# Weighted sum of gathered expert rows: from diagonal matmuls on TensorE to two running sums on VectorE

## The chip, the core and the metric

The kernel runs on one core of a Trainium2 chip. The metric is the device time of one execution in microseconds (us), lower is better. Four engines matter here: TensorE (PE, with its weight loads as PEld), VectorE (DVE), ScalarE (ACT) and GpSimd (POOL). POOL issues the indirect DMAs that gather rows.

## What is computed

Two transformer blocks on 512 tokens of width 1024, in fp32. The change sits in the last part of the first block, a mixture of single-neuron experts (PEER). For each token, product keys pick 8 x 16 = 128 experts with gates; then a dot product with each expert's U row, a gelu, and a weighted sum of the experts' V rows:

```python
def expert_block(args):
    hb, eb, gb = args
    a = jax.nn.gelu(jnp.einsum('td,ted->te', hb, u_tab[eb]).astype(jnp.float32), approximate=False)
    w = (gb * a).astype(hb.dtype)
    return jnp.einsum('te,ted->td', w, v_tab[eb])
```

Every (token, expert) pair needs its own U row and V row: 512 x 128 pairs with 8 KB each.

## The kernel before

The kernel is a row of stages; stage_peer is the one that changes. Tokens are worked on in TB = 4 blocks of P = 128, a token per partition. A block has SLOTS = 128 slots, one for each expert of a token, so there are 512 slots n in all. For slot n one indirect DMA gathers 128 rows of the joined U and V table (1 MB) into entry n % 12 of `uv_ring`; U is the first half of the entry and V the second. The order on each engine is written out by hand and ordered by semaphores:

- **POOL** (L1177 to L1186) issues gather n when s_pv says that slot n - 12 has been added, so its ring entry is free.
- **VectorE** (L1287 to L1305), in each slot n: waits for the gather, multiplies U by the token's row and reduces to one number (L1295, the dot, with a second short instruction that reads the accumulator). In slots with n % 4 = 1 it multiplies the four gelus of the group before by their gates (`weigh`, L1274). Then come a few instructions of the *routing* of the next block (`route`, L1193 to L1260: top-16 searches, and one-hot products of 128x2048 at L1247 to L1253), spread over the first 88 slots of blocks 0 to 2. `gates` (L1262) follows in slot 110, and `update` (L1276), which adds the previous block's result to the residual, in slot 10.
- **ScalarE** (L1327 to L1343), for each group of four slots: the gelu of four dots, then four diagonal matrices `expert_diag` (L1338: identity times the weight column), in a ring of 8.
- **TensorE** (L1366 to L1377), for each slot: two matmuls of diagonal by V (L1372) accumulate in two PSUM banks. The last one releases the ring entry (s_pv). At a block's end ScalarE copies the banks to `out_rows` (L1323), TensorE turns them (L1362), and VectorE's `update` takes the turned tiles from PSUM.

After stage_peer comes the second block of the network (norm, projections, attention, FFN), which needs the last block's `update`.

Of the kernel before, what the change touches and what calls it, by code (L numbers as in the profile page):

```python
# [14 lines left out]
ALU = mybir.AluOpType  # L15
ACT = mybir.ActivationFunctionType
AX_X = mybir.AxisListType.X

P = 128
S = 512  # L20
D = 1024
KD = D // P
TB = S // P
# [9 lines left out]
SLOTS = PEER_H * TOPK  # L33
# [1084 lines left out]
def stage_peer(K):  # L1118
# [3 lines left out]
    nc = K.nc  # L1122
    NT = 2 * PEER_H
    RING = 12
    G = 4
    NGRP = SLOTS // G
    DIAGS = 8
    ROUTE_SLOTS = 88
    EXP_GROUP = 26
    TAIL_SLOT = 110  # L1130
    OUT_SLOT = 10
    with ExitStack() as ctx:
        ring = K.sb(ctx, "uv_ring", [P, RING, 2 * D])
        hN = K.sb(ctx, "h_rows", [P, TB, D])
        xin = K.sb(ctx, "x_again", [P, KD, S])
        oN = K.sb(ctx, "out_rows", [P, D])
# [14 lines left out]
        a = [K.sb(ctx, f"expert_dot{i}", [P, SLOTS]) for i in range(2)]  # L1151
        gl = [K.sb(ctx, f"expert_gelu{i}", [P, SLOTS]) for i in range(2)]
        w = [K.sb(ctx, f"expert_weight{i}", [P, SLOTS]) for i in range(2)]
        diag = [K.sb(ctx, f"expert_diag{i}", [P, P]) for i in range(DIAGS)]
        s_sw = [K.sem(f"route_scores_landed{i}") for i in range(2)]
        s_swf, s_x = K.sem("route_scores_used"), K.sem("x_landed_again")
        s_ht, s_he = K.sem("h_turned"), K.sem("h_rows_copied")
        s_dve, s_d, s_e = K.sem("route_dve"), K.sem("route_diff"), K.sem("route_exp")
        s_idx, s_gate = K.sem("indices_ready"), K.sem("gates_ready")
        s_land = [K.sem(f"rows_landed{r}") for r in range(RING)]  # L1160
        s_dot, s_gelu, s_w, s_diag, s_pv = (
            K.sem("expert_" + n) for n in ("dots", "gelus", "weights", "diagonals", "added"))
        s_oe, s_ot, s_y = K.sem("out_rows_copied"), K.sem("out_turned"), K.sem("x_updated")
        block = ctx.enter_context(nc.Block())

        @block.sync
        def _(sp):
            for tb in range(TB):
                if tb >= 2:
                    sp.wait_ge(s_swf, tb - 1)  # L1170
                sp.dma_start(sw[tb % 2][:, :, :], K.s_dram[tb]).then_inc(s_sw[tb % 2], 16)
                if tb == 1:
                    sp.dma_start(xin[:, :, :], K.x_dram.rearrange("k p s -> p k s")).then_inc(s_x, 16)
# [15 lines left out]
        def _(dve):  # L1189
# [72 lines left out]
            def gates(tb):  # L1262
                dve.wait_ge(s_e, tb + 1)
                g = gate[tb % 2][:, :].rearrange("p (h a) -> p h a", h=PEER_H)
                ch.link(dve.tensor_reduce(den[:, :], g, AX_X, ALU.add))
                ch.link(dve.reciprocal(den[:, :], den[:, :]))
                dve.tensor_tensor(g, g, den[:, :].unsqueeze(2).to_broadcast([P, PEER_H, TOPK]), ALU.mult).then_inc(s_gate, 1)

            def weigh(n):
                tb, g = divmod(n, NGRP)  # L1270
                c = slice(g * G, g * G + G)
                dve.wait_ge(s_gelu, n + 1)
                dve.wait_ge(s_gate, tb + 1)
                dve.tensor_tensor(w[tb % 2][:, c], gl[tb % 2][:, c], gate[tb % 2][:, c], ALU.mult).then_inc(s_w, 1)  # L1274

            def update(tb):  # L1276
                c = slice(tb * P, (tb + 1) * P)
                dve.wait_ge(s_ot, tb + 1)
                if tb == 0:
                    dve.wait_ge(s_x, 16)  # L1280
                for k in range(KD):
                    dve.scalar_tensor_tensor(out=K.hT[:, k, c], in0=K.ps[4 + k // 4][:, (k % 4) * P:(k % 4 + 1) * P],
                                             scalar=K.modT[:, M_GATE2 + k:M_GATE2 + k + 1], in1=xin[:, k, c],
                                             op0=ALU.mult, op1=ALU.add).then_inc(s_y, 1)
            steps = sum(1 for _ in route(0))
            gates(0)
            for tb in range(TB):  # L1287
                ahead, done = (route(tb + 1) if tb + 1 < TB else iter(())), 0
                for s in range(SLOTS):
                    n = tb * SLOTS + s  # L1290
                    if s == 0:
                        dve.wait_ge(s_he, 2 * (tb + 1))
                    dve.wait_ge(s_land[n % RING], 16 * (n // RING + 1))
                    u = ring[:, n % RING, 0:D]
                    dve.tensor_tensor_reduce(u, u, hN[:, tb, :], 1.0, 0.0, ALU.mult, ALU.add,  # L1295
                                             a[tb % 2][:, s:s + 1]).then_inc(s_dot, 1)
                    if n % G == 1 and n > G:
                        weigh(n // G - 1)
                    while done * ROUTE_SLOTS < steps * (s + 1) and done <= steps:
                        next(ahead, None)  # L1300
                        done += 1
                    if s == TAIL_SLOT and tb + 1 < TB:
                        gates(tb + 1)
                    if s == OUT_SLOT and tb:
                        update(tb - 1)  # L1305
            weigh(TB * NGRP - 1)
            update(TB - 1)

        @block.scalar
        def _(act):  # L1310
            def rows(tb):
                for half in range(2):
                    act.wait_ge(s_ht, 2 * tb + half + 1)
                    act.copy(hN[:, tb, 512 * half:512 * half + 512], K.ps[4 + 2 * (tb % 2) + half][:, :]).then_inc(s_he, 1)

            def exps(tb):
                act.wait_ge(s_d, tb + 1)
                act.activation(gate[tb % 2][:, :], top[:, :, :].rearrange("p a b -> p (a b)"), ACT.Exp).then_inc(s_e, 1)

            def out(tb):  # L1320
                act.wait_ge(s_pv, (tb + 1) * SLOTS)
                for half in range(2):
                    act.copy(oN[:, 512 * half:512 * half + 512], K.ps[2 * (tb % 2) + half][:, :]).then_inc(s_oe, 1)  # L1323
            for tb in range(TB):
                rows(tb)
            exps(0)
            for n in range(TB * NGRP):  # L1327
                tb, g = divmod(n, NGRP)
                c = slice(g * G, g * G + G)
                act.wait_ge(s_dot, G * (n + 1))  # L1330
                act.activation(gl[tb % 2][:, c], a[tb % 2][:, c], ACT.Gelu).then_inc(s_gelu, 1)  # L1331
                act.wait_ge(s_w, n + 1)
                for j in range(G):
                    q = n * G + j
                    if q >= DIAGS:
                        act.wait_ge(s_pv, q - DIAGS + 1)
                    s = g * G + j
                    act.activation(diag[q % DIAGS][:, :], K.ident[:, :], ACT.Copy,  # L1338
                                   scale=w[tb % 2][:, s:s + 1]).then_inc(s_diag, 1)
                if g == EXP_GROUP and tb + 1 < TB:  # L1340
                    exps(tb + 1)
                if g == 0 and tb:
                    out(tb - 1)  # L1343
            out(TB - 1)

        @block.tensor
        def _(pe):
            for tb in range(TB):
                for half in range(2):
                    if tb >= 2:  # L1350
                        pe.wait_ge(s_he, 2 * (tb - 2) + half + 1)
                    for k in range(4):
                        last = nc.tensor.transpose(K.ps[4 + 2 * (tb % 2) + half][:, k * P:(k + 1) * P],
                                                   K.hT[:, 4 * half + k, tb * P:(tb + 1) * P], K.ident[:, :])
                    last.then_inc(s_ht, 1)

            def turn(tb):
                pe.wait_ge(s_oe, 2 * (tb + 1))
                if tb:
                    pe.wait_ge(s_y, KD * tb)  # L1360
                for k in range(KD):
                    last = nc.tensor.transpose(K.ps[4 + k // 4][:, (k % 4) * P:(k % 4 + 1) * P],  # L1362
                                               oN[:, k * P:(k + 1) * P], K.ident[:, :])
                last.then_inc(s_ot, 1)
            pe.wait_ge(s_he, 2 * TB)
            for n in range(TB * SLOTS):  # L1366
                tb, s = divmod(n, SLOTS)
                if s == 0 and tb >= 2:
                    pe.wait_ge(s_oe, 2 * (tb - 1))
                pe.wait_ge(s_diag, n + 1)  # L1370
                for half in range(2):
                    last = nc.tensor.matmul(K.ps[2 * (tb % 2) + half][:, :], diag[n % DIAGS][:, :],  # L1372
                                            ring[:, n % RING, D + 512 * half:D + 512 * half + 512],
                                            start=s == 0, stop=s == SLOTS - 1)
                last.then_inc(s_pv, 1)
                if s == G - 1 and tb:
                    turn(tb - 1)  # L1377
            turn(TB - 1)


def stage_in2(K):
# [682 lines left out]
```

## Time and profile before

| | us |
|---|---|
| median of 3 runs (lowest to highest) | 3002.18 (2997.97 to 3004.06) |
| profiled execution, its own time | 2998.2 |
| its span in the trace | 2996.5 |
| first dot starts, last dot starts | 744.2, 2038.1 |
| busy in the whole span: PE, DVE, ACT, POOL | 2280.6, 1359.5, 643.1, 804.3 |

The stage between the first and the last dot takes 1293.9 of the 2996.5 us. The page of the profile gives for each group of instructions the busy time, the mean of one in ns, and the idle time of its engine just before, with what ended it. An engine's busy share over the span says little: stages differ in what limits them.

### The profile page before, as it was taken

Reading aid. Unit: us, or ns where it says so; the run is one execution under the profiler, and the core shown is the slowest. Engines: PE = TensorE matmul, PEld = TensorE weight load, DVE = VectorE, ACT = ScalarE, POOL = GpSimd, SP = SyncE. Lnnn points to the kernel's source line nnn. Section 1 sums busy time; section 2 is a strip of 40 time slices with the busy share of each in tenths; the row PEclk is TensorE's granted clock in tenths of the full one; section 3 lists DMA queues with packets and bytes.
Section 4 is the critical chain, followed back from the end, with each engine's and each line's share of the span. In section 5 each row is a group of like instructions: output and inputs, shape, how many; then the busy total and the mean of one; then the engine's idle time right before and its main releaser. Section 6 shows DMA issues by size and latency. Waiting matters only on the chain. (4 is left out here: it accounts for less than half of the span.)

```text
span 2996.5 us, 21852 instructions
## 1 busy us (share of the span) xinstructions
PE 2280.6 (76%) x6939; PEld 1232.1 (41%) x6939; DVE 1359.5 (45%) x2853; ACT 643.1 (21%) x1374; POOL 804.3 (27%) x618
## 2 busy tenths in 40 slices
PE   4896698670777788777877778785985496799979
PEld 1344343560233333333332333332662242488767
DVE  1107441317667566765677554554144563222200
ACT  1202240200111111112111111113112352255411
POOL 1000000221444444444444444340310000144342
PEclk8897699895899999989899998997996598899989
DMA  6100251333999999999999999993220001133242
GB/s 212 51 14 0 64 162 58 98 91 128 421 420 420 412 420 420 420 386 420 420 420 388 420 420 420 420 420 114 70 88 0 0 1 42 56 98 91 77 116 66
DMA packets 234190, 656.48 MB, mean 219 GB/s; under 512 B 15953, under 2 KB 156796, under 8 KB 168060
## 3 DMA queue, kind: packets, MB, share of 16 engines
q0 software_dynamic: 73728, 536.90, 43.3%
q1 hardware_dynamic: 150416, 110.50, 11.9%
q10 hardware_dynamic: 9966, 8.12, 0.9%
q8 instruction: 36, 0.59, 0.1%
q14 instruction: 44, 0.36, 0.0%
HBM read 645.76 MB, written 9.72 MB: 219 GB/s over the span
## 5 line engine op out<-in xcount | busy, mean ns | idle before, releaser
L1372 PE MATMUL ps<-uv_ring,expert_diag 128*128 128x512 f32 x2048 | 1002.0, 647 | 359.5 <-ACT expert_diag L1338 359.5
L1295 DVE CUSTOM_DVE_ANT_0 uv_ring<-uv_ring,h_rows 128x1024 f32<-128x1024 f32 x512 | 628.9, 1230 | 494.4 <-DMA uv_ring<-in_peer_uv_dram,expert_idx 493.5
L1372 PEld LDWEIGHTS ps<-uv_ring,expert_diag 128*128 128x128 f32 x2048 | 412.5, 207 | 946.5 <-issue 568.5
L1183 POOL DMA_INDIRECT uv_ring<-in_peer_uv_dram,expert_idx x512 | 562.3, 1098 | 814.0 <-PE ps L1372 702.6
L1338 ACT ACTIVATE expert_diag<-ident,expert_weight 128x128 f32<-128x128 f32 x512 | 163.5, 390 | 626.7 <-DVE expert_weight L1274 626.7
L271 POOL TENSOR_TENSOR ffn_low<-ffn_raw,ffn_high 128x1024 fp32r<-128x1024 f32 x44 | 105.2, 2393 | 520.8 <-ACT ffn_high L260 520.8
L271 POOL TENSOR_TENSOR peerq_low<-peerq_raw,peerq_high 128x1024 fp32r<-128x1024 f32 x16 | 38.0, 2380 | 550.8 <-ACT peerq_high L260 550.8
L115 PE MATMUL ps<-ffn_h_high,ffn_high 128*128 128x512 f32 x352 | 139.6, 397 | 18.4 <-POOL ffn_low L271 18.3
L117 PE MATMUL ps<-ffn_h_high,ffn_low 128*128 128x512 f32 x352 | 137.6, 391 | 0.0
L116 PE MATMUL ps<-ffn_h_low,ffn_high 128*128 128x512 f32 x352 | 137.6, 391 | 0.0
L1331 ACT ACTIVATE expert_gelu<-expert_dot 128x4 f32<-128x4 f32 x128 | 26.3, 205 | 490.1 <-DVE expert_dot L1295 490.1
L110 PE MATMUL ps<-hT,in_w 128*128 128x512 f32 x192 | 85.2, 607 | 10.7 <-ACT hT L164 10.7
L1897 DVE TENSOR_TENSOR ffn_prod<-ffn_silu,ps 128x512 f32<-128x512 f32 x22 | 15.2, 689 | 166.4 <-PE ps L117 166.4
L115 PE MATMUL ps<-ff_high,down_high 128*128 128x512 f32 x176 | 69.3, 394 | 20.1 <-POOL down_low L271 20.1
L115 PEld LDWEIGHTS ps<-ffn_h_high,ffn_high 128*128 128x128 f32 x352 | 66.4, 189 | 40.1 <-issue 27.0
L271 POOL TENSOR_TENSOR in_low<-in_raw,in_high 128x1024 fp32r<-128x1024 f32 x16 | 40.8, 2557 | 147.7 <-ACT in_high L260 147.7
L110 PE MATMUL ps<-mix2T,out_w 128*128 128x512 f32 x128 | 56.9, 608 | 22.6 <-DMA out_w<-in_w_out_dram 22.6
L117 PEld LDWEIGHTS ps<-ffn_h_high,ffn_low 128*128 128x128 f32 x352 | 66.5, 189 | 14.2
L116 PEld LDWEIGHTS ps<-ffn_h_low,ffn_high 128*128 128x128 f32 x352 | 66.5, 189 | 13.1
L271 POOL TENSOR_TENSOR down_low<-down_raw,down_high 128x2816 fp32r<-128x2816 f32 x8 | 49.8, 6234 | 78.3 <-ACT down_high L260 78.3
L116 PE MATMUL ps<-ff_low,down_high 128*128 128x512 f32 x176 | 69.0, 392 | 0.0
L117 PE MATMUL ps<-ff_high,down_low 128*128 128x512 f32 x176 | 69.0, 392 | 0.0
(323 smaller groups left out, 2833.5 us busy)
## 6 DMA issues: line engine op xcount, KB each, us to landing
wada_rest<-in_w_ada_dram SPq DMA_DIRECT2D x16, 1024.0 KB, 5.2
ffn_raw<-in_w_gate_dram SPq DMA_DIRECT2D x22, 512.0 KB, 3.8
ffn_raw<-in_w_up_dram SPq DMA_DIRECT2D x22, 512.0 KB, 3.9
down_raw<-in_w_down_dram SPq DMA_DIRECT2D x8, 1408.0 KB, 7.1
wada<-in_w_ada_dram SPq DMA_DIRECT2D x4, 2048.0 KB, 9.5
out_w<-in_w_out_dram SPq DMA_DIRECT2D x8, 1024.0 KB, 5.3
peerq_raw<-in_w_peer_q_dram SPq DMA_DIRECT2D x16, 512.0 KB, 4.0
uv_ring<-in_peer_uv_dram,expert_idx POOLq DMA_INDIRECT x512, 13.7
```

The lines of the kernel that those rows point to most:

```text
L110: return nc.tensor.matmul(out, lhsT, rhs, start=first, stop=last)
L115: nc.tensor.matmul(out, w[0], x[0], start=first, stop=False)
L116: nc.tensor.matmul(out, w[0], x[1], start=False, stop=False)
L117: return nc.tensor.matmul(out, w[1], x[0], start=False, stop=last)
L271: pool.tensor_tensor(self.lo[s][:, :, :], self.raw[s][:, :, :], self.hi[s][:, :, :].bitcast(F32), ALU.subtract).then_inc(self.s_lo[s], 1)
L1183: pool.indirect_dma_start(out=ring[:, n % RING, :], out_offset=None, in_=K.uv, in_offset=bass.IndirectOffsetOnAxis(ap=idx[tb % 2][:, s:s + ...
L1295: dve.tensor_tensor_reduce(u, u, hN[:, tb, :], 1.0, 0.0, ALU.mult, ALU.add, a[tb % 2][:, s:s + 1]).then_inc(s_dot, 1)
L1331: act.activation(gl[tb % 2][:, c], a[tb % 2][:, c], ACT.Gelu).then_inc(s_gelu, 1)
L1338: act.activation(diag[q % DIAGS][:, :], K.ident[:, :], ACT.Copy, scale=w[tb % 2][:, s:s + 1]).then_inc(s_diag, 1)
L1372: last = nc.tensor.matmul(K.ps[2 * (tb % 2) + half][:, :], diag[n % DIAGS][:, :], ring[:, n % RING, D + 512 * half:D + 512 * half + 512], ...
L1897: dve.tensor_tensor(prod[:, :], sl[:, :], K.ps[1][:, :], ALU.mult).then_inc(s_prod, 1)
```

## The change

The diagonals, their matmuls and the PSUM sums go. In their place VectorE itself multiplies each V row by its weight and adds it to one of two SBUF sums (even slots to one, odd slots to the other), five slots behind the dot (LAG = 5). The first add of each sum is a plain multiplication (`tensor_scalar`). After a block's last add VectorE adds the two sums into `out_rows`, and TensorE turns those as before. `update` moves from slot 10 to slot 16. The add, not the matmul, now releases the ring entry to POOL.

```diff
-    DIAGS = 8
+    LAG = G + 1
...
-    OUT_SLOT = 10
+    OUT_SLOT = 16
...
-        diag = [K.sb(ctx, f"expert_diag{i}", [P, P]) for i in range(DIAGS)]
+        acc = [K.sb(ctx, f"expert_sum{i}", [P, D]) for i in range(2)]
...
+            def add(n):
+                tb, s = divmod(n, SLOTS)
+                v, x = ring[:, n % RING, D:2 * D], w[tb % 2][:, s:s + 1]
+                dve.wait_ge(s_w, n // G + 1)
+                if s < 2:
+                    if tb:
+                        dve.wait_ge(s_oe, tb)
+                    ins = dve.tensor_scalar(acc[s % 2][:, :], v, x, None, ALU.mult)
+                else:
+                    dve.wait_ge(s_pv, n - 1)
+                    ins = dve.scalar_tensor_tensor(out=acc[s % 2][:, :], in0=v, scalar=x, in1=acc[s % 2][:, :],
+                                                   op0=ALU.mult, op1=ALU.add)
+                ins.then_inc(s_pv, 1)
+                if s == SLOTS - 1:
+                    if tb:
+                        dve.wait_ge(s_ot, tb)
+                    dve.wait_ge(s_pv, n + 1)
+                    dve.tensor_tensor(oN[:, :], acc[0][:, :], acc[1][:, :], ALU.add).then_inc(s_oe, 1)
+
...
                     if n % G == 1 and n > G:
                         weigh(n // G - 1)
+                    if n >= LAG:
+                        add(n - LAG)
...
             weigh(TB * NGRP - 1)
+            for n in range(TB * SLOTS - LAG, TB * SLOTS):
+                add(n)
             update(TB - 1)
...
-                act.wait_ge(s_w, n + 1)
-                for j in range(G):
-                    q = n * G + j
-                    if q >= DIAGS:
-                        act.wait_ge(s_pv, q - DIAGS + 1)
-                    s = g * G + j
-                    act.activation(diag[q % DIAGS][:, :], K.ident[:, :], ACT.Copy,
-                                   scale=w[tb % 2][:, s:s + 1]).then_inc(s_diag, 1)
...
-            for n in range(TB * SLOTS):
-                tb, s = divmod(n, SLOTS)
-                if s == 0 and tb >= 2:
-                    pe.wait_ge(s_oe, 2 * (tb - 1))
-                pe.wait_ge(s_diag, n + 1)
-                for half in range(2):
-                    last = nc.tensor.matmul(K.ps[2 * (tb % 2) + half][:, :], diag[n % DIAGS][:, :],
-                                            ring[:, n % RING, D + 512 * half:D + 512 * half + 512],
-                                            start=s == 0, stop=s == SLOTS - 1)
-                last.then_inc(s_pv, 1)
```

VectorE's queue in four slots of the routing part of a block, before (L1295 is the dot and its accumulator read, L1274 is `weigh`, L1204 and L1212 to L1220 are routing):

```order
L1204 MAX_INDEX route_idx<-route_max,route_scores 128x8 x2
L1295 ISA uv_ring,expert_dot<-uv_ring,h_rows 128x1024
L1295 ISA expert_dot 128x1
L1274 TENSOR_TENSOR expert_weight<-expert_gelu,expert_gate 128x4
L1204 MAX_INDEX route_idx<-route_max,route_scores 128x8
L1295 ISA uv_ring,expert_dot<-uv_ring,h_rows 128x1024
L1295 ISA expert_dot 128x1
L1204 MAX_INDEX route_idx<-route_max,route_scores 128x8
```

The same kind of place now (L1313 is the dot, L1273 `weigh`, L1285 the add, L1224 and L1230 routing):

```order
L1313 ISA uv_ring,expert_dot<-uv_ring,h_rows 128x1024
L1313 ISA expert_dot 128x1
L1285 SCALAR_TENSOR_TENSOR expert_sum<-uv_ring,expert_weight,expert_sum 128x1024
L1230 MATCH_REPLACE route_cand<-route_top,route_cand 128x256 x2
L1313 ISA uv_ring,expert_dot<-uv_ring,h_rows 128x1024
L1313 ISA expert_dot 128x1
L1273 TENSOR_TENSOR expert_weight<-expert_gelu,expert_gate 128x4
L1285 SCALAR_TENSOR_TENSOR expert_sum<-uv_ring,expert_weight,expert_sum 128x1024
L1230 MATCH_REPLACE route_cand<-route_top,route_cand 128x256
```

Each slot has gained one VectorE instruction of 128x1024 between its dot and its routing work. At the end of the stage VectorE's queue now reads as follows (L1292 adds the two sums, L1300 is `update`):

```order
L1313 ISA uv_ring,expert_dot<-uv_ring,h_rows 128x1024
L1313 ISA expert_dot 128x1
L1285 SCALAR_TENSOR_TENSOR expert_sum<-uv_ring,expert_weight,expert_sum 128x1024
L1273 TENSOR_TENSOR expert_weight<-expert_gelu,expert_gate 128x4
L1285 SCALAR_TENSOR_TENSOR expert_sum<-uv_ring,expert_weight,expert_sum 128x1024 x5
L1292 TENSOR_TENSOR out_rows<-expert_sum 128x1024
L1300 SCALAR_TENSOR_TENSOR hT<-ps,modT,x_again 128x128 x8
```

Before, nothing but `weigh` and the eight of `update` stood behind the last dot on this engine. On TensorE the stage changes like this:

```order
-L1353 MATMUL ps<-ident,hT 128x128 x32
-L1372 MATMUL ps<-uv_ring,expert_diag 128x512 x264
-L1362 MATMUL ps<-ident,out_rows 128x128 x8
-L1372 MATMUL ps<-uv_ring,expert_diag 128x512 x256
-L1362 MATMUL ps<-ident,out_rows 128x128 x8
...
+L1360 MATMUL ps<-ident,hT 128x128 x32
+L1370 MATMUL ps<-ident,out_rows 128x128 x32
```

Only the turning of rows stays on TensorE during the stage.

## Rows read from the trace of the kernel before

**Rows 1.** Page, groups of instructions: busy, mean ns | idle before, releaser.

```profile
L1372 PE MATMUL ps<-uv_ring,expert_diag 128*128 128x512 f32 x2048 | 1002.0, 647 | 359.5 <-ACT expert_diag L1338 359.5
L1295 DVE CUSTOM_DVE_ANT_0 uv_ring<-uv_ring,h_rows 128x1024 f32<-128x1024 f32 x512 | 628.9, 1230 | 494.4 <-DMA uv_ring<-in_peer_uv_dram,expert_idx 493.5
L1183 POOL DMA_INDIRECT uv_ring<-in_peer_uv_dram,expert_idx x512 | 562.3, 1098 | 814.0 <-PE ps L1372 702.6
```

**Rows 2.** Stretches of the stage: PE, PEld, DVE, ACT, POOL busy, PEclk, DMA share, GB/s.

```profile
1000.00:1100.00 100.00, 78.35 (x168) 32.81 (x168) 56.20 (x120) 18.66 (x55) 41.51 (x40) 0.93 1.01 420
1300.00:1400.00 100.00, 79.90 (x163) 33.27 (x164) 54.00 (x103) 18.98 (x57) 43.34 (x40) 0.91 0.97 397
1600.00:1700.00 100.00, 76.65 (x158) 32.16 (x159) 64.36 (x109) 17.71 (x53) 45.40 (x39) 0.90 0.97 396
```

**Rows 3.** Timeline of DVE, four dots: start, us, instruction, idle before and releaser.

```profile
1499.56 1.23 DVE L1295 CUSTOM_DVE_ANT_0 uv_ring<-uv_ring,h_rows 128x1024 f32<-128x1024 f32 x1 [0.78 <-DMA uv_ring<-in_peer_uv_dram,expert_idx]
...
1507.04 1.23 DVE L1295 CUSTOM_DVE_ANT_0 uv_ring<-uv_ring,h_rows 128x1024 f32<-128x1024 f32 x1 [0.69 <-DMA uv_ring<-in_peer_uv_dram,expert_idx]
```

**Rows 4.** Timeline of DVE where landed rows had piled up.

```profile
1303.50 1.22 DVE L1295 CUSTOM_DVE_ANT_0 uv_ring<-uv_ring,h_rows 128x1024 f32<-128x1024 f32 x1
1304.65 0.08 DVE L1295 DVE_READ_ACCUMULATOR2_ANT expert_dot<- 128x1 f32 x1
1304.65 1.22 DVE L1295 CUSTOM_DVE_ANT_0 uv_ring<-uv_ring,h_rows 128x1024 f32<-128x1024 f32 x1
...
1306.94 0.15 DVE L1274 TENSOR_TENSOR expert_weight<-expert_gelu,expert_gate 128x4 f32<-128x4 f32 x1
1307.02 1.22 DVE L1295 CUSTOM_DVE_ANT_0 uv_ring<-uv_ring,h_rows 128x1024 f32<-128x1024 f32 x1
```

**Rows 5.** DVE instructions nearest to the add: groups and one merged timeline row.

```profile
2068.68 5.39 DVE L158 SCALAR_TENSOR_TENSOR X<-hT,vecT,rs_in 128x512 f32<-128x512 f32 x8
L158 DVE SCALAR_TENSOR_TENSOR X<-hT,vecT,rs_in x8: 743/744/750, 2068.7 to 2073.3; 128x512 f32<-128x512 f32 x8
L727 DVE TENSOR_TENSOR gla_qe<-qkT,gla_e x7: 1208/1216/1224, 256.1 to 289.5; 128x1024 f32<-128x1024 f32 x7
L311 DVE TENSOR_TENSOR ffn_h_low<-hT,ffn_h_high 128x512 fp32r<-128x512 f32 x8 | 4.9, 686 | 0.9 <-ACT ffn_h_high L306 0.9
L934 DVE TENSOR_SCALAR swa_p<-swa_p,swa_sum x32: 346/351/354, 357.7 to 436.3; 128x256 f32<-128x256 f32 x32
```

**Rows 6.** DVE groups in 975.5:1301, block 1 from its first dot.

```profile
L1295 DVE CUSTOM_DVE_ANT_0 uv_ring<-uv_ring,h_rows 128x1024 f32<-128x1024 f32 x128 | 157.2, 1230 | 109.8 <-DMA uv_ring<-in_peer_uv_dram,expert_idx 109.7
L1265 DVE TENSOR_REDUCE route_den<-expert_gate 128x8 f32<-128x128 f32 x1 | 0.3, 286 | 0.5 <-ACT expert_gate L1318 0.5
```

**Rows 7.** Timeline: a routing step that waits for the one before it.

```profile
1300.67 0.29 DVE L1258 SCALAR_TENSOR_TENSOR expert_idxf<-route_e 128x128 f32<-128x128 f32 x1
1301.00 0.23 DVE L1260 CAST expert_idx<-expert_idxf 128x128 uint32<-128x128 f32 x1
```

**Rows 8.** The gather's source line on POOL: ns min/median/max, and issue to landing.

```profile
L1183 POOL DMA_INDIRECT uv_ring<-in_peer_uv_dram,expert_idx x512: 935/940/3040, 736.6 to 2022.4; - x171
DMA to landing us min/median/max: 5.6/13.7/20.5
```

**Rows 9.** Timelines of POOL and DVE: gathers issued during VectorE's work.

```profile
882.51 1.43 POOL L1183 DMA_INDIRECT uv_ring<-in_peer_uv_dram,expert_idx  x1 [5.43 <-PE ps L1372]
...
881.90 1.23 DVE L1295 CUSTOM_DVE_ANT_0 uv_ring<-uv_ring,h_rows 128x1024 f32<-128x1024 f32 x1 [0.99 <-DMA uv_ring<-in_peer_uv_dram,expert_idx]
883.06 2.29 DVE L1212 TENSOR_TENSOR route_cand<-route_max 128x2048 f32<-128x2048 f32 x1
...
1282.10 3.04 POOL L1183 DMA_INDIRECT uv_ring<-in_peer_uv_dram,expert_idx  x1 [1.78 <-PE ps L1372]
...
1282.04 2.29 DVE L1247 TENSOR_TENSOR route_scores<-route_cf,iota 128x2048 f32<-128x2048 f32 x1
...
1504.56 0.94 POOL L1183 DMA_INDIRECT uv_ring<-in_peer_uv_dram,expert_idx  x1 [0.47 <-PE ps L1372]
...
1504.54 1.27 DVE L1295 CUSTOM_DVE_ANT_0 uv_ring<-uv_ring,h_rows 128x1024 f32<-128x1024 f32 x1 [1.05 <-DMA uv_ring<-in_peer_uv_dram,expert_idx]
```

**Rows 10.** Timelines of ACT, PE and DVE at the stage's end.

```profile
2048.96 1.07 ACT L1323 COPY out_rows<-ps 128x512 f32<-128x512 f32 x2 [7.88 <-PE ps L1372]
2050.08 1.09 PE L1362 MATMUL ps<-ident,out_rows 128*128 128x128 f32 x8 [1.17 <-ACT out_rows L1323]
2051.21 2.16 DVE L1282 SCALAR_TENSOR_TENSOR hT<-ps,modT,x_again 128x128 f32<-128x128 f32 x8 [11.45 <-PE ps L1362]
```

**Rows 11.** Stretches with an idle PE, PE alone: busy, PEclk, DMA share, GB/s.

```profile
690.00:740.00 50.00, 0.00 (x0) 0.50 0.10 34
2050.00:2052.00 2.00, 1.09 (x8) 1.00 0.00 0
2055.40:2057.00 1.60, 1.60 (x2) 0.50 0.94 204
```

More of the change, by code:

```diff
@@ L1160, in stage_peer @@
         s_land = [K.sem(f"rows_landed{r}") for r in range(RING)]
-        s_dot, s_gelu, s_w, s_diag, s_pv = (
-            K.sem("expert_" + n) for n in ("dots", "gelus", "weights", "diagonals", "added"))
-        s_oe, s_ot, s_y = K.sem("out_rows_copied"), K.sem("out_turned"), K.sem("x_updated")
+        s_dot, s_gelu, s_w, s_pv = (K.sem("expert_" + n) for n in ("dots", "gelus", "weights", "added"))
+        s_oe, s_ot, s_y = K.sem("out_rows_summed"), K.sem("out_turned"), K.sem("x_updated")
         block = ctx.enter_context(nc.Block())
@@ L1318, in exps @@
                 act.activation(gate[tb % 2][:, :], top[:, :, :].rearrange("p a b -> p (a b)"), ACT.Exp).then_inc(s_e, 1)
-            def out(tb):
-                act.wait_ge(s_pv, (tb + 1) * SLOTS)
-                for half in range(2):
-                    act.copy(oN[:, 512 * half:512 * half + 512], K.ps[2 * (tb % 2) + half][:, :]).then_inc(s_oe, 1)
             for tb in range(TB):
@@ L1331, in _ @@
                 act.activation(gl[tb % 2][:, c], a[tb % 2][:, c], ACT.Gelu).then_inc(s_gelu, 1)
-                act.wait_ge(s_w, n + 1)
-                for j in range(G):
-                    q = n * G + j
-                    if q >= DIAGS:
-                        act.wait_ge(s_pv, q - DIAGS + 1)
-                    s = g * G + j
-                    act.activation(diag[q % DIAGS][:, :], K.ident[:, :], ACT.Copy,
-                                   scale=w[tb % 2][:, s:s + 1]).then_inc(s_diag, 1)
                 if g == EXP_GROUP and tb + 1 < TB:
                     exps(tb + 1)
-                if g == 0 and tb:
-                    out(tb - 1)
-            out(TB - 1)
         @block.tensor
@@ L1355, in _ @@
                     last.then_inc(s_ht, 1)
-            def turn(tb):
-                pe.wait_ge(s_oe, 2 * (tb + 1))
+            pe.wait_ge(s_he, 2 * TB)
+            for tb in range(TB):
+                pe.wait_ge(s_oe, tb + 1)
                 if tb:
@@ L1364, in turn @@
                 last.then_inc(s_ot, 1)
-            pe.wait_ge(s_he, 2 * TB)
-            for n in range(TB * SLOTS):
-                tb, s = divmod(n, SLOTS)
-                if s == 0 and tb >= 2:
-                    pe.wait_ge(s_oe, 2 * (tb - 1))
-                pe.wait_ge(s_diag, n + 1)
-                for half in range(2):
-                    last = nc.tensor.matmul(K.ps[2 * (tb % 2) + half][:, :], diag[n % DIAGS][:, :],
-                                            ring[:, n % RING, D + 512 * half:D + 512 * half + 512],
-                                            start=s == 0, stop=s == SLOTS - 1)
-                last.then_inc(s_pv, 1)
-                if s == G - 1 and tb:
-                    turn(tb - 1)
-            turn(TB - 1)
 def stage_in2(K):
```

## The prediction

> **What bounds the stage now.** I read the page's groups first. The diagonal matmuls are the costliest group of the whole program, with 1002.0 us busy, and that invites the guess that taking them away gains much. The idle column says otherwise [rows 1]: VectorE's dots waited 493.5 us, all of it for gathers; POOL waited 702.6 us for the matmuls, which is no more than a full ring. The stretches settle it [rows 2]: the DMA engines are busy all the time (share 1.01, 420 GB/s), with two dips to 0.97. In steady state three dots are 7.48 us apart, 2.49 us a slot [rows 3], and 1 MB at 420 GB/s is 2.5 us. So DMA bandwidth bounds the stage, and 512 slots x 2.49 = 1275 of its 1293.9 us are bandwidth. Nothing that TensorE gives back can make it shorter. What matters is whether VectorE, which had 110 us of slack in a block of 325.5 us [rows 6], can carry the adds below the 2.49.
>
> **VectorE's new load.** I count by pitch (start to start), since instructions overlap: an instruction's duration is some 0.08 more than its pitch.
> - A dot: with rows piled up, 1303.50 to 1304.65, pitch 1.15 with its accumulator read; `weigh` has 0.08 [rows 4]. Over the three dots from 1303.50 to 1306.94 it is 1.147, which I use.
> - An add: scalar_tensor_tensor of 128x1024 from SBUF isn't in the trace. The same operation at 128x512 takes 744 ns, and eight take 5.39, so its pitch is (5.39 - 0.74) / 7 = 0.664 [rows 5]. From 512 to 1024 elements tensor_tensor goes from 686 to 1216 ns, 0.53 more. So the add has a pitch of 0.664 + 0.53 = 1.20. Bounds: below, the tensor_tensor of 128x1024, 1.216 - 0.08 = 1.14; above, two of 128x512, 1.33. I take 1.20, since the operation is the same and the slope is plain. The first add of each sum is a tensor_scalar: 351 ns for 256 elements where tensor_tensor would have some 0.42, so it runs at two elements at a time; I put it at 0.67, eight times.
> - `weigh` is now followed by an add that needs its result. A step that waits for the one before starts 0.33 after it where that took 0.29 [rows 7], so `weigh` (0.16) costs 0.20 in place of 0.08: 0.12 more, in every fourth slot.
> - The final addition of a block: 1.22 less the overlap, with the wait in front some 1.33.
>
> A slot without routing is thus 1.147 + 1.20 + 0.20 / 4 = 2.40 us, just below DMA's 2.49. With routing it is above.
>
> **Other work on VectorE.** Block 1 lasts 325.5 us from its first dot, less 110.3 idle = 215.2 occupied [rows 6]. Less 128 dots (146.8) and less some 10 for the overlap that a queue without gaps saves (0.08 in each slot), 58 are left for routing, `weigh` issue, `update` and `gates`. In the 88 routing slots that is near 0.6 a slot: 3.0 us against DMA's 2.49. So blocks 0 to 2 become VectorE's.
>
> **The sum from the first dot to the last.** 511 dots x 1.147 = 586.1; 506 adds (498 x 1.20 + 8 x 0.67) = 603.0; other work 3 x 58 = 174, less an `update` that block 0 lacks (2.1), plus `weigh` and `update` of block 3 (4.7) = 176.6; waits behind `weigh` 127 x 0.12 = 15.2; three final additions 4.0. Together 1384.9. The first five slots have no add and stay with DMA: 5 x (2.49 - 1.75) = +3.7. At the other end, from slot 88 of block 2 on, 168 slots have no routing and DMA is the slower by 0.09 to 0.10 each, 16.3. The rows landed ahead pay part of it: a ring entry is released 2.35 after the dot five slots on has started, the issue may have to wait some 1.1 for a dot (below), and issue to landing takes at least 5.6 [rows 8], so gather n + 12 lands some 9.0 after dot n + 5 starts, and is needed 7 slots or 16.8 after: 7.8 to spare. VectorE's final addition, `update` and `gates` there (4.5) count against it too, so 16.3 - 7.8 - 4.5 = +4. Sum: 1392.6 against 1293.9, **+98.7**.
>
> **The end.** Before, 13.1 us from the last dot's start (2038.1) to `update` (2051.21): TensorE worked off its backlog, ScalarE copied the banks, TensorE turned them in 1.09 [rows 10]. Now: dot 1.15, add 1.20, `weigh` 0.20, five adds 6.0, final addition 1.33, and the turning. TensorE has rested by then, and in a stretch without matmuls its granted clock is 0.50, that is 1.2 in place of 2.4 GHz, where the turning before had 1.00 [rows 11]; so I double it to 2.2, with 0.1 of handing over. 12.2 us: **-0.9**. The matmuls that come next started at 0.50 before as well [rows 11], so nothing changes for them. Turnings of blocks 0 to 2 have eleven slots of cover before `update`. ScalarE's lost 164 us were covered by the DMA wait and give nothing; its gelus can only come sooner.
>
> +98.7 - 0.9 = +97.8 on the profiled 2998.2 gives 3096. The runs' median is 4 above the profiled execution: **3100 us**.
>
> **A rule weighed.** VectorE and POOL meet [rows 9]. A gather issued during a dot (882.51, dot until 883.13) ends at 883.94, 0.81 after the dot, in place of taking 0.94; one issued at 1282.10 under a routing product until 1284.33 ends at 1285.14, again 0.81 after. The median issue is 940 ns, the longest 3040 [rows 8]. So POOL waits for a VectorE instruction with two SBUF inputs to end, and it slips in between that and the next, even where they overlap (883.06). In the other direction the dot of 1504.54, begun with a gather's issue, took 1.27 in place of 1.23. Hence now: an entry is released at an add's end, the issue is held by the following dot and ends about 2.0 after the release, inside the 2.4 of a slot. VectorE loses at most 0.04 a slot, 20 us in all if it always met; this is part of my upper bound.
> The Trainium skill's page "SBUF — State Buffer", section "SBUF: two separate sides", says that whichever of the two starts first has the shared pair for its whole instruction and the other fully blocks. For POOL waiting the trace agrees; for VectorE waiting it shows 0.04 and not the 0.94 of an issue. By that rule each issue could stop VectorE for some 0.8 us.
>
> **Rivals.**
> 1. *Adds hidden, on the other side: no change or a small gain.* If the add ran like the tensor_scalar (0.67), a slot would be 1.147 + 0.67 + 0.05 = 1.87, with routing 2.5 on average, and DMA would bind everywhere. Then the two dips (3% of 100 us each) and some 3 us at the end come back: about 2994. It decides if the pitch of an add is below about 0.75. Against it: 744 ns for 512 elements of the same operation [rows 5]. 3%.
> 2. *VectorE stopped by each issue* (the lock in both directions): 512 x 0.8 = 410, about 3510. Against it: the dot that met an issue took 1.27, not 2.0 [rows 9]. 3%.
> 3. *POOL starved.* Between an add and the next dot there is no accumulator read; if POOL could not slip in there or missed its one gap, an issue would wait for two instructions, as the 3.04 of 1282.10 [rows 9], and the 3.5 us period would outlast the slot in the 248 slots without routing. With a pace between 2.4 and 3.5, say 3.0: 248 x 0.6 = 149, about 3250. 6%.
> 4. *Dearer adds or stretched dots*: pitch 1.33 gives 498 x 0.13 = 65 less the 4 at the end, 3160; stretched dots give 3120. 12%.
> The rest, 76%, is the forecast. Its own range: with adds at 1.14 VectorE saves 30, but DMA then binds more at the end (168 x 0.16 = 27, less 7 and 4.5, is 15 in place of 4), so 3081; above, 3130.
>
> **Range and chances.** 3070 to 3165 takes in the forecast, both bounds of the add and rival 4; rivals 1 to 3 stay outside with 12%. About 0.2% (6 us) is what a measurement of this kernel tells from no change. Slower: rivals 2 to 4 and the forecast, 97%; rival 1 is split, 1% faster and 2% the same.
>
> **What would show it.** Right: add rows of about 1.28 us; in the first 88 slots of blocks 0 to 2 no idle time before dots and a slot of 3.0, DMA share there near 0.83; later slots at 2.40, turning to 2.49 with waits for DMA late in block 3; POOL issues near 2.0 us; granted clock 0.50 throughout. Wrong: adds of 0.7 us (rival 1), VectorE instructions of about 2 us (rival 2), or dots that wait for gathers while the DMA share is well below 1 (rival 3).

## The result

| | us |
|---|---|
| before, median of 4 runs (lowest to highest) | 3001.53 (2997.97 to 3004.06) |
| changed kernel, median of 4 runs (lowest to highest) | 3100.82 (3098.41 to 3101.39) |
| ratio, 95% interval | 1.033 (1.0312 to 1.0348) |
| forecast | 3100 (3070 to 3165), slower with 97% |
| profiled execution, its own time and span | 3101.39, 3099.6 |

The kernel became 3.3% slower, as forecast. The page of the changed kernel, its groups of instructions (busy, mean ns | idle before, releaser), beside [rows 1]:

```profile
L1182 POOL DMA_INDIRECT uv_ring<-in_peer_uv_dram,expert_idx x512 | 788.1, 1539 | 693.2 <-DVE expert_sum L1285 574.3
L1285 DVE SCALAR_TENSOR_TENSOR expert_sum<-uv_ring,expert_weight,expert_sum 128x1024 f32<-128x1024 f32 x504 | 645.1, 1281 | 4.4
L1313 DVE CUSTOM_DVE_ANT_0 uv_ring<-uv_ring,h_rows 128x1024 f32<-128x1024 f32 x512 | 621.5, 1214 | 18.7 <-DMA uv_ring<-in_peer_uv_dram,expert_idx 14.9
L1370 PE MATMUL ps<-ident,out_rows 128*128 128x128 f32 x32 | 7.8, 426 | 1460.4 <-DVE out_rows L1292 1460.4
```

Read the idle columns. The dots' wait for gathers has gone from 493.5 to 14.9 us: VectorE is now the engine that is waited for. TensorE's 1002 us of matmuls are gone and the engine idles; no time came back for it. The stretches of block 2's routing part, of its other 40 slots, and of block 3 (PE, PEld, DVE, ACT, POOL busy, PEclk, DMA share, GB/s), beside [rows 2]:

```profile
1462.70:1724.40 261.70, 1.97 (x8) 1.57 (x8) 260.43 (x501) 4.52 (x22) 127.86 (x89) 0.50 0.95 365
1724.40:1823.50 99.10, 0.00 (x0) 0.00 (x0) 98.61 (x136) 4.93 (x13) 64.13 (x40) 0.50 0.96 391
1823.50:2141.90 318.40, 1.97 (x8) 1.57 (x8) 311.14 (x424) 6.37 (x31) 209.74 (x122) 0.50 0.99 412
```

In the first, VectorE is busy for 260.43 of 261.70 us and the gathers come at 365 in place of 420 GB/s. From the dots' starts in the timeline: the routing parts of blocks 0 to 2 take 257.7, 261.6 and 261.6 us where they took 227.4, 228.5 and 228.1; the 40 slots behind each take 99.2 against 97.1 to 97.4. Block 3, during which VectorE has no routing to do, takes the same 318.4 from first to last dot in both kernels. So all of the loss, 103.0 us between first and last dot, lies in blocks 0 to 2.

The timeline of VectorE in slots without routing, and then POOL's row there:

```profile
1402.23 1.22 DVE L1313 CUSTOM_DVE_ANT_0 uv_ring<-uv_ring,h_rows 128x1024 f32<-128x1024 f32 x1
1403.38 0.08 DVE L1313 DVE_READ_ACCUMULATOR2_ANT expert_dot<- 128x1 f32 x1
1403.38 1.28 DVE L1285 SCALAR_TENSOR_TENSOR expert_sum<-uv_ring,expert_weight,expert_sum 128x1024 f32<-128x1024 f32 x1
1404.58 1.22 DVE L1313 CUSTOM_DVE_ANT_0 uv_ring<-uv_ring,h_rows 128x1024 f32<-128x1024 f32 x1
...
1402.59 1.68 POOL L1182 DMA_INDIRECT uv_ring<-in_peer_uv_dram,expert_idx  x1 [0.67 <-DVE expert_sum L1285]
```

Dot pitch 1.15, add pitch 1.20, no gap. The add before this dot ended at 1402.32; the issue starts 0.27 later, is held until the dot ends at 1403.45, and ends 0.82 behind it, still inside the slot's 2.35.

At the stage's end (DVE and PE timelines), beside [rows 10]:

```profile
2144.30 6.06 DVE L1285 SCALAR_TENSOR_TENSOR expert_sum<-uv_ring,expert_weight,expert_sum 128x1024 f32<-128x1024 f32 x5
2150.47 1.23 DVE L1292 TENSOR_TENSOR out_rows<-expert_sum 128x1024 f32<-128x1024 f32 x1
2153.76 2.16 DVE L1300 SCALAR_TENSOR_TENSOR hT<-ps,modT,x_again 128x128 f32<-128x128 f32 x8 [2.06 <-PE ps L1370]
...
2151.75 1.97 PE L1370 MATMUL ps<-ident,out_rows 128*128 128x128 f32 x8 [312.90 <-DVE out_rows L1292]
```

From the last dot (2141.9) to `update` 11.9 us, where it was 13.1. The turning took 1.97 in place of 1.09, at a granted clock of 0.50.

### The profile page after: what moved, and what is told of

Its sections match the earlier page's. It is cut to its first block and busy times, and to the rows that moved or that the text cites. A ratio compares the mean times of both kernels' runs of the same rounds, so it can differ in the third digit from the quotient of the medians.

```text
span 3099.6 us, 18137 instructions
## 1 busy us (share of the span) xinstructions
PE 1283.5 (41%) x4891; PEld 822.6 (27%) x4891; DVE 1943.4 (63%) x3369; ACT 475.4 (15%) x854; POOL 1030.1 (33%) x618
## 5 line engine op out<-in xcount | busy, mean ns | idle before, releaser
L1182 POOL DMA_INDIRECT uv_ring<-in_peer_uv_dram,expert_idx x512 | 788.1, 1539 | 693.2 <-DVE expert_sum L1285 574.3
L1285 DVE SCALAR_TENSOR_TENSOR expert_sum<-uv_ring,expert_weight,expert_sum 128x1024 f32<-128x1024 f32 x504 | 645.1, 1281 | 4.4
L1313 DVE CUSTOM_DVE_ANT_0 uv_ring<-uv_ring,h_rows 128x1024 f32<-128x1024 f32 x512 | 621.5, 1214 | 18.7 <-DMA uv_ring<-in_peer_uv_dram,expert_idx 14.9
L1370 PE MATMUL ps<-ident,out_rows 128*128 128x128 f32 x32 | 7.8, 426 | 1460.4 <-DVE out_rows L1292 1460.4
L1370 PEld LDWEIGHTS ps<-ident,out_rows 128*128 128x128 f32 x32 | 6.3, 223 | 1461.8 <-DVE out_rows L1292 1030.6
```

The lines of the kernel that those rows point to most:

```text
L1182: pool.indirect_dma_start(out=ring[:, n % RING, :], out_offset=None, in_=K.uv, in_offset=bass.IndirectOffsetOnAxis(ap=idx[tb % 2][:, s:s + ...
L1285: ins = dve.scalar_tensor_tensor(out=acc[s % 2][:, :], in0=v, scalar=x, in1=acc[s % 2][:, :], op0=ALU.mult, op1=ALU.add)
```

## Experiments

Two theories at first. **A**: VectorE's occupied time in the routing parts is the whole loss. **B**: the loss comes from the new path of release and issue, where most gathers' issues are held by a dot (the median one takes 1.68 in place of 0.94 us). Every kernel below starts from the changed kernel unless it says otherwise; each ratio is to the kernel before on the same chip.

**noroute** leaves out the routing of blocks 1 to 3, so that they work with block 0's experts and gates.

```diff
+                if tb:
+                    for _ in range(100):
+                        yield
+                    ch.link(dve.tensor_copy(cf[:, 0, 0:8], mif[:, 0, 0, 0:8]))
+                    dve.tensor_copy(cf[:, 0, 8:16], mif[:, 0, 0, 0:8]).then_inc(s_d, 1)
+                    dve.tensor_copy(cf[:, 0, 16:24], mif[:, 0, 0, 0:8]).then_inc(s_swf, 1)
+                    dve.wait_ge(s_swf, tb + 1)
+                    dve.tensor_copy(idx[tb % 2][:, :], idxf[:, :]).then_inc(s_idx, 1)
+                    return
```

> The changed kernel with the routing of blocks 1 to 3 left out (they use the experts and gates of block 0; four tiny copies keep the semaphores going). Adds, releases and gathers are as in the changed kernel. Theory A (VectorE's occupied time in the routing parts of blocks 0 to 2 is the whole loss): a slot needs 2.40 us of VectorE against 2.50 of DMA, so every block falls back to the 320 us of block 3 and the time to about 2987 us (2980 to 2994), a little below the kernel before. Theory B (the slower path of release and issue, gathers held up by VectorE's two-input instructions, is the loss): that path is untouched, so about 3100.

Measured: 2997.48 us, ratio 0.9986 (0.9977 to 0.9996). The whole loss is gone although all adds and the release path are there. The gather's source line and its landing times (ns min/median/max; us):

```profile
L1182 POOL DMA_INDIRECT uv_ring<-in_peer_uv_dram,expert_idx x512: 932/1786/1977, 736.7 to 2024.4; - x171
DMA to landing us min/median/max: 7.5/14.7/20.1
```

The issues are held as long as in the changed kernel (median 1786 against 1677 ns), and it costs nothing: theory B falls. The gathers of this kernel fetch the same rows in every block; width8 below does without that. A stretch of this kernel, its block 2:

```profile
1393.80:1718.05 324.25, 1.97 (x8) 1.57 (x8) 314.50 (x433) 9.45 (x35) 216.26 (x128) 0.50 1.01 416
```

DMA is busy throughout, and the block still takes 324 us, not the 320 I expected. So DMA's own pace is 324.25 / 128 = 2.53 a slot, not 2.49, and some 2997 us is what this way of gathering gives at DMA's pace. My 2987 (2980 to 2994) missed by that.

**width768, width512, width8** do the add on fewer columns; the rest of the sum is left out.

```diff
-                    ins = dve.scalar_tensor_tensor(out=acc[s % 2][:, :], in0=v, scalar=x, in1=acc[s % 2][:, :],
+                    ins = dve.scalar_tensor_tensor(out=acc[s % 2][:, 0:768], in0=v[:, 0:768], scalar=x, in1=acc[s % 2][:, 0:768],
```

> The changed kernel with each add done on 768 of its 1024 columns (the rest of the sum is left out). Theory A: the add's pitch falls by 256 x 1.04 ns = 0.27 to 0.93. The routing part of a block goes from 261.6 to 238 us, against DMA's 220; the 40 slots after it are DMA's (100) less some 8 for rows landed ahead, so a block takes 330, three take 991 against 975.5 before: 3014 us (3008 to 3025). Theory B: unchanged, since each release is still followed by a dot that holds the issue: near 3100.

> The changed kernel with each add done on 512 of its 1024 columns. Theory A: pitch 0.66, a routing slot 2.97 - 0.53 = 2.44, just under DMA's 2.50: the loss is gone, about 2991 us (2985 to 3000). Theory B: near 3100.

> The changed kernel with each add done on 8 of its 1024 columns, so that VectorE's load is nearly that of before, while TensorE still does no sums. Both theories: DMA bounds everything. Blocks near 320 us in place of 325, and an end that is shorter by six adds: about 2984 us (2978 to 2991). If it stayed at 3000 or above, something of the loss would come from TensorE's absence or from the order of releases.

| columns | us | ratio, 95% | routing part, block 2 | the 40 slots behind |
|---|---|---|---|---|
| 1024 | 3100.82 | 1.033 (1.0312 to 1.0348) | 261.6 | 99.2 |
| 768 | 3028.15 | 1.0093 (1.0076 to 1.011) | 240.4 | 96.5 |
| 512 | 3006.20 | 1.0023 (1.0013 to 1.0033) | 233.6 | 95.5 |
| 8 | 2997.07 | 0.9991 (0.9982 to 1.0001) | 231.3 | 95.1 |

From 1024 to 768 columns an add is 0.27 us shorter (1281 to 1014 ns), and 88 x 0.267 = 23 us a routing part are expected where 21 were measured: time follows VectorE's work nearly one for one. Further down it flattens: a routing part with the 40 slots behind it takes 329 and 326 us, near DMA's 324. The figures as expected were 14, 15 and 13 us too low, all three outside their ranges, in good part because a block needs 324 us of DMA and not 320.

The 2997 of width8 hides something. Its last dot starts at 2042.0, 3.9 us later than in the kernel before (2038.1), and its blocks 0 to 2 take 979.7 us (975.5 before, 973.7 in noroute); an end that is 5.7 us shorter, with its short adds, makes up for it. So VectorE's work is shown to be all but some 4 to 6 of the 103 us. What these few are, the 0.22 us that even an add of 8 columns takes, the order of the releases or something else, is open.

**tscalar** makes every add a tensor_scalar, without accumulation.

```diff
-                    ins = dve.scalar_tensor_tensor(out=acc[s % 2][:, :], in0=v, scalar=x, in1=acc[s % 2][:, :],
-                                                   op0=ALU.mult, op1=ALU.add)
+                    ins = dve.tensor_scalar(acc[s % 2][:, :], v, x, None, ALU.mult)
```

> The changed kernel with every add a tensor_scalar of all 1024 columns (the accumulation is left out): the price that the first rival put on the add. I expect 0.75 us for one, a pitch of 0.67, VectorE below DMA in every slot and about 2992 us (2985 to 3000). If an instruction that runs at two elements at a time kept POOL out for longer than its own duration, waits for gathers would appear and the time would be above 3010.

Measured: 3005.17 us, 1.0021 (1.0012 to 1.0031). Groups of this kernel:

```profile
L1285 DVE TENSOR_SCALAR expert_sum<-uv_ring,expert_weight 128x1024 f32<-128x1024 f32 x504 | 377.3, 749 | 4.4
```

and of width512:

```profile
L1285 DVE SCALAR_TENSOR_TENSOR expert_sum<-uv_ring,expert_weight,expert_sum 128x512 f32<-128x512 f32 x504 | 376.6, 748 | 4.4
```

The 2992 (2985 to 3000) expected was 13 us too low, as in width512 and for the same reason. Two different instructions of the same 0.75 us give the same time within some 1 us: what counts here is the duration on VectorE, and not whether the instruction reads one or two tensors from SBUF. It also shows that the first rival was a real one with a real price: with adds of pitch 0.67 the change would have cost 0.2% and not 3.3%, though it would not have gained (the rival had 2994).

**route112** spreads routing over 112 slots.

```diff
-    ROUTE_SLOTS = 88
-    EXP_GROUP = 26
-    TAIL_SLOT = 110
+    ROUTE_SLOTS = 112
+    EXP_GROUP = 29
+    TAIL_SLOT = 124
```

> The changed kernel with the routing spread over 112 in place of 88 slots of a block (exps and gates later too). Theory A says that the sum of VectorE's work in a block counts, 361 against 320 us, not its peaks: the same time, 3100 us (3095 to 3103), perhaps 2 less because only 144 in place of 168 slots without routing are left to DMA's slower pace. A theory by which the heaviest slots cost (the ring running empty there) expects a gain of 10 us or more.

Measured: 3096.45 us, 1.0325 (1.0308 to 1.0342). Blocks 1 and 2 take 361.1 us each, where they took 360.8 in the changed kernel. Where VectorE sets the pace throughout, only the sum of its work counts, not how it is spread. Of the 4 us that came back only 1.6 lie between first and last dot: block 3 takes 3.2 less (315.2), where 2 less were expected, and blocks 0 to 2 take 1.6 more. The others lie ahead of the first dot and behind the last.

**lag7, lag9** widen LAG; the diff of lag9 (lag7 has G + 3):

```diff
-    LAG = G + 1
+    LAG = G + 5
```

> The changed kernel with LAG = 7: five slots, 12.5 us, are left for the 9.0 of release, issue and landing, 3.5 us to spare in place of 8. The rows landed ahead that pay for the end are fewer, so DMA binds some 5 us earlier in block 3: 3106 us (3102 to 3115).

> The changed kernel with LAG = 9 in place of 5: an entry is released 9 slots behind its dot, so only 3 slots are left for issue and landing. By the sum of the prediction a gather lands 9.0 us after the dot with which its entry's release began, so 3 slots must last 9.0: a slot of 3.0 everywhere, also in the 248 slots without routing, 0.5 to 0.6 more each: about 3250 us (3220 to 3290). If release and issue had much more room than that sum says, the time would stay within 10 us of 3101.

Measured: lag7 3104.22 us, 1.0348 (1.0331 to 1.0365), as expected. lag9 3388.44, 1.1289 (1.127 to 1.1308), far above the 3250 (3220 to 3290) expected. Its source lines of the dot and the gather:

```profile
L1313 DVE CUSTOM_DVE_ANT_0 uv_ring<-uv_ring,h_rows x512: 1195/1224/1291, 745.0 to 2427.0; 128x1024 f32<-128x1024 f32 x171
...
L1182 POOL DMA_INDIRECT uv_ring<-in_peer_uv_dram,expert_idx x512: 932/937/2747, 738.2 to 2420.3; - x171
DMA to landing us min/median/max: 5.3/6.9/20.0
```

A slot is (2427.0 - 745.0) / 511 = 3.29, three are 9.9. And its timeline:

```profile
2204.18 1.22 DVE L1313 CUSTOM_DVE_ANT_0 uv_ring<-uv_ring,h_rows 128x1024 f32<-128x1024 f32 x1 [1.34 <-DMA uv_ring<-in_peer_uv_dram,expert_idx]
2205.33 0.08 DVE L1313 DVE_READ_ACCUMULATOR2_ANT expert_dot<- 128x1 f32 x1
2205.33 1.28 DVE L1285 SCALAR_TENSOR_TENSOR expert_sum<-uv_ring,expert_weight,expert_sum 128x1024 f32<-128x1024 f32 x1
2206.88 0.94 POOL L1182 DMA_INDIRECT uv_ring<-in_peer_uv_dram,expert_idx  x1 [2.83 <-DVE expert_sum L1285]
```

From the dot's start to the issue 2.70, and from the issue to landing 6.9 in the median, at a rate of 317 GB/s (2010 to 2420 us) and so with no full queue ahead: 9.6, where I had 9.0 with the shortest landing, 5.6. Of the 288 us, the 248 slots without routing account for 248 x (3.29 - 2.49) = 198, and the 264 with routing, which at 2.97 I had thought nearly covered by a loop of 3.0, for 264 x (3.29 - 2.97) = 84. The loop as a mechanism is shown; its length was mis-sized.

**smooth512, smoothbefore.** What are width512's 9 us above the 2997 of noroute and width8? Either routing's peaks (**C**: its last six instructions of 2.3 us stand in four slots) or VectorE's sum (**D**). The edit puts four steps between the six; smoothbefore has the same in the kernel before.

```diff
-                    yield
+                    for _ in range(4):
+                        yield
                     ch.link(dve.tensor_tensor(pick, cf[:, c, :].unsqueeze(2).to_broadcast([P, SLOTS, TOPK]),
...
```

> width512 with routing's six instructions of 2.3 us, which stood in four slots at the end of the routing part, set four steps apart, so over some 14 slots. width512 took 3006 us, 9 above the floor of 2997 that noroute and width8 share. Theory C (the 9 us are these peaks: for 4 slots VectorE needs near 5 us each, more than the rows landed ahead cover, and DMA idles): now the ring covers them, 2999 us (2996 to 3002). Theory D (the 9 us are the sum of VectorE's work in the routing part): unchanged, 3006.

> The kernel before with the same spreading of routing's six instructions of 2.3 us, everything else as it was. Its blocks 0 to 2 take 324.5 to 325.9 us where DMA alone needs 324 (noroute). If its two dips in DMA share come from the peaks, some 1 to 1.5 us a block come back: 2998 us, a ratio of 0.999, which is hardly measurable; more than 0.2% can't come back, since 2997 is the floor. If the dips are DMA's own pauses, no change.

Measured: smooth512 3000.87 us, 0.9996 (0.9982 to 1.0009); smoothbefore 2995.93 us, 0.9982 (0.9968 to 0.9997). One stretch of width512:

```profile
1600.00:1700.00 100.00, 0.00 (x0) 0.00 (x0) 90.30 (x154) 4.93 (x13) 49.61 (x38) 0.50 0.95 383
```

and the same of smooth512:

```profile
1600.00:1700.00 100.00, 0.00 (x0) 0.00 (x0) 86.89 (x141) 4.93 (x13) 51.10 (x41) 0.50 1.00 402
```

The dip is gone, and 5 of the 9 us with it: C holds for the larger part. In the traces blocks 0 to 2 take 979.4 us in place of 985.4; that is where width8 stands too (979.7), so the rest isn't the width of the adds. Where VectorE has slack on average, its peaks count; where it has none, they don't (route112). smoothbefore is the only kernel of this study that computes the whole result and comes out below the kernel before: its blocks 0 to 2 take 972.8 us together in place of 975.5, 0.9 a block, a little less than expected. At 0.2%, with an interval that ends at 0.9997, it is near the limit of what can be told. Its 2995.93 also lies below the 2997 that I had called a floor: that figure is good to some microseconds and no hard limit.

## Why the prediction was right

- **DMA bounds the stage before.** Right: noroute and width8, whose VectorE work differs widely, both end at 2997 us, a match that holds to some 5 us only (width8, above). TensorE's 1002 us were worth nothing: without them the last dots start at 2039.1 and 2042.0, where it was 2038.1. The pace was mis-sized: 2.49 holds between neighbours, 2.53 over a block.
- **The add's price**, pitch 1.20 from a 128x512 row and a slope: 1.20, duration 1.28. A tensor_scalar of 1024 columns takes 0.75 us, a pitch of 0.67 as extrapolated.
- **A slot**: 2.40 forecast; 2.39 measured behind the routing (three of 2.34 and one of 2.54 with `weigh`). With routing 3.0 forecast, 2.97 measured. The window of [rows 6] is not quite what its heading says: block 1 of the kernel before starts at 1068.7, and 975.5:1301 runs from slot 89 of block 0 to slot 89 of block 1. Block 1 itself takes 325.8 us with 111.0 idle, against 325.5 and 110.3 there, so the sum that rests on it stands.
- **First to last dot**: 1392.6 forecast, 1396.9 measured, and the sum hides two misses of opposite sign. Up to slot 88 of block 2 I had 1392.6 - 409 = 984 (167 x 2.40 + 8.5 being the 409); 979.4 was measured: blocks 1 and 2 took 360.8 us each where the terms add up to 363.6 (128 x 2.347 + 58 + 32 x 0.12 + 1.33). The last stretch took 417.5 (1724.36 to 2141.9), 8 more than the 409. The failed term is the "+4 at the other end". The dots turn to DMA's pace at slot 35 of block 3, 75 slots behind the routing, where that term has (7.8 + 4.5) / 0.097 = 127. With the measured numbers it nearly closes: DMA needs 167 x 2.53 = 422.5; rows landed ahead spare 16.8 less 2.35 (dot and add), 0.27 (hand over), 0.75 (held issue) and 6.9 (landing, from lag9), 6.5 us; 416.0 in all.
- **Luck in the last digits.** Between the two profiled executions lie 103.2 us (2998.2 to 3101.39), where 97.8 were forecast. The 4 us then added from the profiled execution to the median hold for the kernel before (3.3 with its four runs), but the changed kernel's median lies 0.6 below its profiled execution, which is the highest of the four. So 3100 for 3100.82 owes some 5 us to chance; the mechanism and the size of the loss don't.
- **The end**: -0.9 forecast, -1.2 measured. TensorE's rest cost 0.9 in the turning; from `update` on the rest of the program takes 945.8 us, where it was 945.3.
- **The rule weighed.** POOL waits for VectorE as [rows 9] showed: an issue ended 1.95 after its release, 2.0 was forecast. The other direction didn't appear: dots take 1214 ns on average in place of 1230, so not even the 0.04 was there, and rival 2 is out. A dot that started 0.57 us into an issue took 1.23 all the same:

```profile
2028.13 0.94 POOL L1182 DMA_INDIRECT uv_ring<-in_peer_uv_dram,expert_idx  x1 [0.86 <-DVE expert_sum L1285]
2028.70 1.23 DVE L1313 CUSTOM_DVE_ANT_0 uv_ring<-uv_ring,h_rows 128x1024 f32<-128x1024 f32 x1 [0.84 <-DMA uv_ring<-in_peer_uv_dram,expert_idx]
```

  The Trainium skill's page "SBUF — State Buffer", section "SBUF: two separate sides", says that the one that starts first has the pair for its whole instruction; for VectorE held by an issue the traces show the opposite. Nor did rival 3 show: no issue waited for two instructions. The longest took 2.75 us, begun under a routing product of 2.28 and ended 0.81 behind it.
- **A sign that misled**: I expected a DMA share of 0.83 in the routing parts. The rate is 365 of 420 GB/s, 0.87, but the share reads 0.95. In the rows above, the share falls more slowly than the rate: 1.01 at 416 GB/s, 0.96 at 391, 0.95 at 365. Why isn't shown; the rate is the safer figure.

## What to carry to other kernels

Busy time that is taken off an engine is worth what the resource that sets the stage's pace waits for it, here nothing; the question to ask is what the work costs where it lands. Put the receiving engine's pitch per item beside the pace-setting resource's pitch per item, part by part: 2.40 against 2.53 was free, 2.97 against 2.53 cost 34 us a block, though on the mean over the whole kernel before VectorE was only 45% busy (1359.5 of 2996.5 us). Then check peaks only where there is slack on average, and the loop of a ring (release, issue, landing) with the typical landing, not the shortest.

## What the runs showed of the hardware

- In steady gathering the dots of noroute are 2.49 apart, and once in some 72 us they are 3.47 apart:

```profile
1910.02 1.23 DVE L1322 CUSTOM_DVE_ANT_0 uv_ring<-uv_ring,h_rows 128x1024 f32<-128x1024 f32 x1
1912.51 1.23 DVE L1322 CUSTOM_DVE_ANT_0 uv_ring<-uv_ring,h_rows 128x1024 f32<-128x1024 f32 x1
1915.98 1.23 DVE L1322 CUSTOM_DVE_ANT_0 uv_ring<-uv_ring,h_rows 128x1024 f32<-128x1024 f32 x1 [0.84 <-DMA uv_ring<-in_peer_uv_dram,expert_idx]
```

  The same happened at 1839.2 and 1983.3. The extra 0.98 us in 28 or 29 slots is the difference of 2.49 and 2.53 (0.034 a slot). The DMA share shows no gap there (421 GB/s in 1912.5 to 1916). The rate does sag for some microseconds in each of the three periods from 1840 on, as to 351 GB/s in 1939.75 to 1941.50; whether that is the same event, and what causes it, stays open.
- A gather of 1 MB with no full queue ahead (lag9, 317 GB/s) lands 6.9 us after its issue in the median, 5.3 the shortest. The median is 4.4 more than the 2.5 us that 1 MB takes at 420 GB/s.
- Whether a dot holds an issue depends on which started when. In the trace of the kernel before, 170 issues that started 0.05 to 1.09 us after a dot's start all ended 0.81 us behind its end. 50 issues that started within 0.04 us of a dot's start were not held at all (0.94 us), and these dots took 1.26 to 1.29 us in place of 1.23; the pair at 1504.54 in [rows 9] is one of them. The prediction took this pair for the price of any meeting.
